# A decoder trunk's experts: copying the summed rows to the outputs before the last two blocks are added

## The reference, cut to what matters

```python
def moe(h, blk, w_router, router_bias, w_e_gate, w_e_up, w_e_down, w_s_gate, w_s_up, w_s_down):
    hf = h.reshape(B * S, D)
    eidx, gw = route(hf, w_router, router_bias)          # top 8 of 64 experts for each row
    routed = routed_experts(hf, eidx, gw, w_e_gate, w_e_up, w_e_down, blk)
    shared = swiglu(hf, w_s_gate, w_s_up, w_s_down)
    return (routed + shared).astype(h.dtype).reshape(B, S, D)

# routed_experts: pairs (row, expert) are sorted by expert and cut into blocks of one expert;
# a block's rows are gathered, go through its SwiGLU, are scaled by their weights and added:
    out = jnp.zeros((M + 1, D), ys.dtype).at[row_tok].add(ys * row_w[:, None])
```

## Time and profile before

| | |
|---|---|
| median of 3 runs | 2251.98 us (2250.02 to 2253.24) |
| span of the profiled execution | 2244.9 us |
| time around the span (median less span) | 7.1 us |
| busy: PE, DVE, ACT, POOL | 2097, 1345, 1050, 1023 us |
| experts' phase | from 1335.3 to 2244.9 us, 66 blocks |
| mean granted TensorE clock | 0.974 of full speed |

### The profile page before, as it was taken

One profiled execution on the slowest core, in us unless ns is written; L12 is line 12 of the kernel. 1 busy time (PEld: TensorE's weight loads), 2 busy tenths in 40 slices (PEclk: granted clock), 3 DMA queues, 4 the chain that ended last, 5 costly groups with the idle time before them and its releaser, 6 DMA issues. The chain is left out here.

```text
span 2244.9 us, 42905 instructions
## 1 busy us (share of the span) xinstructions
PE 2097.4 (93%) x15302; PEld 1583.8 (71%) x15302; DVE 1344.5 (60%) x2337; ACT 1050.3 (47%) x1584; POOL 1023.4 (46%) x850
## 2 busy tenths in 40 slices
PE   7998989979799989999898989999999999999994
PEld 6776767757444448888687647777777777777773
DVE  4478767675576662111357537777777777777772
ACT  6321213266566661111243216666666666666662
POOL 2111213252577741111015614567776676667662
PEclk9999999989899999999999999999999999999997
DMA  6577821064655556983342259999999999999996
GB/s 224 163 250 241 271 74 38 27 208 128 204 168 168 165 172 229 302 274 103 131 148 95 96 218 323 335 337 338 336 331 340 338 336 335 338 338 337 335 327 156
DMA packets 178690, 520.62 MB, mean 232 GB/s; under 512 B 22907, under 2 KB 77354, under 8 KB 152142
## 3 DMA queue, kind: packets, MB, share of 16 engines
q1 hardware_dynamic: 130070, 355.43, 45.2%
q0 software_dynamic: 37520, 97.81, 17.0%
q10 hardware_dynamic: 10992, 66.02, 8.7%
HBM read 442.31 MB, written 125.08 MB: 253 GB/s over the span
## 5 line engine op out<-in xcount | busy, mean ns | idle before, releaser
L2724 DVE TENSOR_TENSOR w_gu_lo<-turned,w_gu_hi 128x2048 fp32r<-128x2048 f32 x132 | 302.6, 2293 | 146.8 <-ACT w_gu_hi L2646 146.8
L2646 ACT ACTIVATE w_gu_hi<-turned 128x2048 fp32r<-128x2048 f32 x132 | 253.9, 1924 | 38.2 <-PEq L1926 38.2
L623 PE MATMUL pP<-wring,hT_hi 128*128 128x512 f32 (+1 forms) x576 | 225.9, 392 | 26.2 <-DVE wring L549 22.2
L625 PE MATMUL pP<-wring,hT_lo 128*128 128x512 f32 (+1 forms) x576 | 221.7, 385 | 0.0
L624 PE MATMUL pP<-wring,hT_hi 128*128 128x512 f32 (+1 forms) x576 | 221.4, 384 | 0.0
L2573 PE MATMUL pG_e<-w_gu_hi,xT_hi 128*128 128x512 f32 x528 | 214.7, 407 | 0.0
L2573 PE MATMUL pG_e<-w_gu_lo,xT_hi 128*128 128x512 f32 x528 | 209.0, 396 | 0.0
L2573 PE MATMUL pG_e<-w_gu_hi,xT_lo 128*128 128x512 f32 x528 | 208.6, 395 | 0.0
L2500 POOL DMA_INDIRECT x_scratch<-turned,target x66 | 106.8, 1619 | 205.9 <-ACT turned L2687 205.9
L389 POOL TENSOR_TENSOR wring<-turned,wring 128x512 fp32r<-128x512 f32 (+1 forms) x43 | 69.0, 1634 | 232.0 <-ACT wring L423 231.6
L2486 POOL DMA_INDIRECT turned<-h_scratch,index x64 | 159.0, 2484 | 20.0 <-issue 20.0
(11 more groups left out here) (335 smaller groups left out, 5030.3 us busy)
## 6 DMA issues: line engine op xcount, KB each, us to landing
turned<-in_w_e_up SPq DMA_DIRECT2D x65, 1024.0 KB, 11.2
turned<-in_w_e_down SPq DMA_DIRECT2D x65, 1024.0 KB, 6.8
turned<-in_cache_sb_kv SPq DMA_DIRECT2D x256, 256.0 KB, 3.1
turned<-in_w_e_gate SPq DMA_DIRECT2D x64, 1024.0 KB, 7.1
out<-in_cache_win_kv ACTq DMA_DIRECT2D x8, 4094.0 KB
turned<-in_w_in ACTq DMA_DIRECT2D x56, 256.0 KB, 7.0
turned<-in_w_in SPq DMA_DIRECT2D x16, 512.0 KB, 7.1
out<-in_cache_win_kv ACTq DMA_DIRECT2D x8, 1022.0 KB
```

The lines of the kernel that those rows point to most:

```text
L623: pe.matmul(pP[:m, i % 4, :w], hi, w_hi(u), start=(c == 0), stop=False)
L625: last = pe.matmul(pP[:m, i % 4, :w], lo, w_hi(u), start=False, stop=(c == KC - 1))
L2646: act.activation(ghi[:, r, k, :, :].rearrange("p c f -> p (c f)"), w[:, r, k, :], ACT.Copy).then_inc(ghi_ready, 1)
L2724: dve.tensor_tensor(glo[:, r, k, :, :].rearrange("p c f -> p (c f)"), w[:, r, k, :], ghi[:, r, k, :, :].rearrange("p c f -> p (c f)").bitc ...
```

## The change

The last two blocks (the last turn) are no longer added to x2 but to the outputs. SP waits only for `y_out` of the turns before (`last * 64`), and then issues all three copies of x2 to the outputs, both halves of the prompt among them; ACT issues none and waits for none.

POOL adds the last two blocks with a new `scatter_last`. The first of them waits for `copied` (48), the second for all of the first block's transfers. Each issues four indirect adding DMAs: rows and quarter rows to y_prompt, with bounds (an index from S on is skipped), and rows and quarter rows to y_sample, with indices that are smaller by S, where those of prompt rows have been pushed out of bounds by adding 65536. Padding slots are out of bounds in all four. The shifted indices are in a new SBUF tensor, `slot_decode`, which DVE computes at the end of `phase_out_route` with four instructions on 128 x 116 elements; POOL copies a block's pair of them to `target_decode` in a further small copy beside `aim`. The last block's results go to buffers of their own (`y_end`, `tail_end`, which are the row buffers of even blocks, free by then), so ACT's last put waits for no landing. A block of the last turn now adds 64 to `y_out`.

The diff, cut to its core:

```diff
@@ phase_out_route
+        beyond = sb("beyond", [P, 2, NBLK])
...
                     dve.tensor_tensor(x2[:m, t % 2, :], pY[:m, t % 2, :], x1_row(t), ALU.add).then_inc(x2_ready, 1)
+                for n, rows in enumerate((S, QT * S)):
+                    index = pT[:, n * P:n * P + NBLK]
+                    chain(dve.tensor_scalar(beyond[:, n, :], index, float(rows), float(FAR), ALU.is_lt, ALU.mult))
+                    chain(dve.scalar_tensor_tensor(slot_decode[:, :, n], index, -float(rows), beyond[:, n, :], ALU.add, ALU.add))
@@ phase_experts, SP
-                sp.wait_ge(y_out, last * (U * 32) + U * 32)
+                sp.wait_ge(y_out, last * (U * 32))
                 sp.dma_start(o[1][:, 0], sc["x2"][S:T, :]).then_inc(copied, 16)
-                sp.dma_start(half_rows(o[0][0], 0), half_rows(sc["x2"], 0)).then_inc(copied, 16)
+                for h in range(2):
+                    sp.dma_start(half_rows(o[0][0], h), half_rows(sc["x2"], h)).then_inc(copied, 16)
+                sp.wait_ge(y_out, last * (U * 32) + U * 64)
+                sp.nop(nofuse=True)
                 sp.wait_ge(copied, 48)
@@ POOL
+                def scatter_last(it, j):
+                    src, src_tail = (y, y_tail) if j == 0 else (y_end, tail_end)
+                    aim(it, j)
+                    pool.tensor_copy(target_decode[:, j, :], slot_decode[:, bass.ds(it * U + j, 1), :]).then_inc(decode_ready, 1)
+                    pool.wait_ge(target_ready, it * U + (j + 1))
+                    pool.wait_ge(decode_ready, j + 1)
+                    pool.wait_ge(y_copied, it * (2 * U) + 2 * (j + 1))
+                    if j == 0:
+                        pool.wait_ge(copied, 48)
+                    else:
+                        pool.wait_ge(y_out, it * (U * 32) + 64 * j)
+                    pool.nop(nofuse=True)
+                    for dst, at, rows_at, part in ((o[0][0], target, S, src), (out_quarters, target, QT * S, src_tail),
+                                                   (out_decode, target_decode, NS, src), (decode_quarters, target_decode, QT * NS, src_tail)):
+                        k = 1 if part is src_tail else 0
+                        pool.indirect_dma_start(dst, bass.IndirectOffsetOnAxis(ap=at[:, j, k:k + 1], axis=0), part, None,
+                                                bounds_check=rows_at - 1, oob_is_err=False, compute_op=ALU.add).then_inc(y_out, 16)
...
-                for n in range(LAG):
+                for n in range(1, LAG):
                     for j in range(U):
-                        aim(last - (LAG - 1 - n), j)
-                        scatter(last - (LAG - 1 - n), j)
-                pool.wait_ge(y_out, last * (U * 32) + U * 32)
+                        aim(last - n, j)
+                        scatter(last - n, j)
+                for j in range(U):
+                    scatter_last(last, j)
+                pool.wait_ge(y_out, last * (U * 32) + U * 64)
@@ ACT
+                def put_end(it):
+                    j = U - 1
+                    act.wait_ge(y_ready, it * U + (j + 1))
+                    act.wait_ge(target_ready, it * U + (j + 1))
+                    act.activation(y_end, pY[:, :], ACT.Copy, scale=scale[:, j % 2, 2:3]).then_inc(y_copied, 1)
+                    act.activation(tail_end, pQ[:, :QW], ACT.Copy, scale=scale[:, j % 2, 3:4]).then_inc(y_copied, 1)
...
-                put(last, U - 1)
-                act.wait_ge(y_out, last * (U * 32) + U * 32)
-                act.dma_start(half_rows(o[0][0], 1), half_rows(sc["x2"], 1)).then_inc(copied, 16)
-                act.wait_ge(copied, 48)
+                put_end(last)
```

More of the change, by code:

```diff
@@ L47 @@
 BIG = 1e30
+FAR = 1 << 16
 GATE_RING = 3
@@ L165, in build @@
             branches.close()
-            phase_out_route(nc, a, o, scratch, ident, turned, expert_row, slot_info)
-            phase_experts(nc, a, o, scratch, ident, turned, expert_row, slot_info)
+            slot_decode = attention.enter_context(nc.sbuf_tensor("slot_decode", [P, NBLK, 2], I32))
+            phase_out_route(nc, a, o, scratch, ident, turned, expert_row, slot_info, slot_decode)
+            phase_experts(nc, a, o, scratch, ident, turned, expert_row, slot_info, slot_decode)
 def phase_project(nc, a, o, sc, ident, turned):
@@ L1760, in expert_weights, with phase_out_route @@
     return a[name][0].rearrange("e (p c) f -> e p (c f)", p=P)[bass.ds(e, 1)].rearrange("e p n -> (e p) n")
-def phase_out_route(nc, a, o, sc, ident, turned, expert_row, slot_info):
+def phase_out_route(nc, a, o, sc, ident, turned, expert_row, slot_info, slot_decode):
     NC = T // 3
@@ L2343, in _, with phase_experts @@
                     dve.tensor_tensor(x2[:m, t % 2, :], pY[:m, t % 2, :], x1_row(t), ALU.add).then_inc(x2_ready, 1)
+                for n, rows in enumerate((S, QT * S)):
+                    index = pT[:, n * P:n * P + NBLK]
+                    chain(dve.tensor_scalar(beyond[:, n, :], index, float(rows), float(FAR), ALU.is_lt, ALU.mult))
+                    chain(dve.scalar_tensor_tensor(slot_decode[:, :, n], index, -float(rows), beyond[:, n, :], ALU.add, ALU.add))
                 dve.wait_ge(slots_ready, 4)
                 dve.wait_ge(row_ready, 2)
-def phase_experts(nc, a, o, sc, ident, turned, expert_row, slot_info):
+def phase_experts(nc, a, o, sc, ident, turned, expert_row, slot_info, slot_decode):
     U = TURN
@@ L2376, in phase_experts @@
         scale = target[:, :, :].bitcast(F32)
+        target_decode = sb("target_decode", [P, 2, 2], I32)
+        y_end, tail_end = rows[0], tail[0]
         xhi = sb("xT_hi", [P, 2, KC, P], F32R)
@@ L2420, in phase_experts @@
         copied = sem("c_copied")
+        decode_ready = sem("c_decode_ready")
+        out_quarters = o[0][0].rearrange("t (q n) -> (t q) n", q=QT)
+        out_decode = o[1].rearrange("t n d -> (t n) d")
+        decode_quarters = o[1].rearrange("t n (q d) -> (t n q) d", q=QT)
         def half_rows(ap, h):
```

## The result

| | before | after |
|---|---|---|
| median | 2253.3 us (20 runs) | 2259.15 us (20 runs) |
| ratio | | 1.0024, 95% interval 1.0018 to 1.0031 |
| span of the profiled execution | 2244.9 us | 2256.9 us |
| a block in the experts' loop | 13.247 us | 13.313 us |
| from block B's second scatter to the end | 41.1 us | 43.8 us |

The changed kernel is 5.4 us slower (0.0024 x 2253.3). The forecast was 2250.7 us, 1.3 us less than before. The profiled executions differ by 12.0 us: 5.2 of it is there already at the first block's gate (1349.8 us in before, 1354.9 us here), 4.1 comes in the loop over the blocks, 2.6 behind block B. The other two stay.

What follows compares the result with a forecast made beforehand. The end was taken as bound by the drain after PE's last matmul, 27.8 us of landings, POOL issues and copy. Drain sum 2242.8 plus 0.8 for bounds gave span 2243.6, plus 7.1 around it 2250.7 us; range 2246 to 2257.

Steps and rivals of the forecast that it cites:

- Step 1: In the final drain, SP issues the copy of x2 at 2208.7, 20.9 us earlier; it lands at 2223.8.
- Step 2: POOL waits for the copy's landing, so C, the second-to-last block, starts at 2224.6, 10.8 us later than before.
- 3, C's last transfer: On POOL, four transfers per block in place of two, spaced 1.88 us: 3.76 us more, for each last block.
- step 5: Pause from C's last start to D's (last block's) first: 3.69 us, POOL's aims just hidden, ACT's put off the path.
- 4, D landed: Each last block's final, nearly empty transfer lands 2.88 us after its start.
- Step 7: Check of bounds on POOL: 0.1 us more for each of eight transfers, 0.8 together, giving a span of 2243.6 us.
- Step 6: Sum of the drain: D's last transfer at 2239.6, landed 2242.5, end of span 2242.8 us.
- Step 8: Phase before the experts: DVE's four added instructions, some 1.6 us, are hidden under the last x2 row's store.
- rival of traffic: Skipped rows still cost DMA time as if moved, both last blocks DMA-bound: 4.1 us slower, 2256.1 us; chance 0.06.
- the faster: Rival: skipped rows are nearly free on POOL in the last blocks' transfers: span 2238.9, 2246.0 us; chance 0.15.
- slower rival: Bounded transfers take POOL 0.6 us longer each, eight on the path, with high landings: 2258.7 us; chance 0.17.
- the sign by which the prediction was to fail as a whole: POOL's cost per bounded transfer differs by more than 0.8 us from that of the unbounded one.

Runs made afterwards that it cites:

- e3: Kernel before with only the three new SBUF tensors allocated in their places, unused: 2255.76 us, ratio 1.0011, 13.313 us a block.
- e9: Changed kernel with slot_decode at the top of SBUF and target_decode behind all other tensors, so no tile moves: 2256.18 us, ratio 1.0005.
- e4: Changed kernel with POOL's aims of both last blocks ahead of the wait for the copy: 2258.65 us, ratio 1.0022 to the kernel before.
- e11: As e9, but without the four transfers to y_sample: 2252.25 us, ratio 0.9988 to the kernel before.
- e8: Changed kernel without POOL's own wait for the last landings: 2258.67 us, ratio 1.0020 to the kernel before.
- e10: As e9, with both aims early, no last wait on POOL, and D's first two transfers waiting only for C's first two: 2253.36 us, ratio 1.0000.

## Why the prediction was wrong

Against block B's second scatter (2203.81 in before, 2213.11 in after), the steps compare as follows.

| step | forecast | measured in after |
|---|---|---|
| 1, copy issued | 4.9 | 4.7 |
| 1, copy landed | 20.0 | 20.7 |
| 2, block C starts | 20.8 | 21.5 |
| 3, C's last transfer | 26.4 | 27.1 |
| 5, block D starts | 30.1 | 31.4 |
| 3, D's last transfer | 35.8 | 37.0 |
| 4, D landed | 38.6 | 39.7 |
| 7, check of bounds | 0.8 | 0 |
| 6, end of the span | 39.8 | 43.8 |

- Step 6 failed. "End of span" was put 0.37 us behind the last landing, because it is so in before. There, the last thing to land is a copy issued by SP and ACT, and POOL's drain of 3.49 us had ended 11 us before that. With POOL's own transfers last, the drain is exposed: 4.1 us from landing to end. This is 3.7 of the 4.0 us by which the end was missed. What step 5 names for the pause, "what is late next", no step names for the end of the kernel: the trace had the drain's length (L2430), and it was not read. It is a cover that was taken away unseen, while the copy it lay under was moved.
- The loop's 2.6 to 4.1 us were missed altogether. Step 8 is right about DVE: DVE's four instructions start at 1336.57 and the last ends at 1337.8, and ACT starts the experts 3.45 us behind the start of L2346, as 1331.88 and 1335.33 are apart in the earlier trace rows. But the prediction puts the two new tensors' place in SBUF at nothing, without a reason; its sign for step 8, that before 2200 no time should change, did fire. The allocation moved the tiles of the loop that PE bounds (e3, e9).
- Step 5 erred by 0.55 us. The sentence that ACT's put leaves the path was wrong: the put needs the second `aim` (it scales by its weights), and POOL got to that only behind C's transfers. Step 2 asked what is queued behind POOL's new wait, named the transfers, and forgot the aim and with it ACT. With the aim ahead, the pause is 3.52 us (e4), where 3.69 was forecast. The added small copy does not take as long again as the first, as step 5 has it: it starts 0.12 us behind it (2241.34 against 2241.22), which was not on the path.
- Step 1 was right in place and 0.8 us short in size: the copy took 15.97 us in place of 15.15, and 15.5 to 16.5 in the repeats, over the 16 us of its own sign in four of seven (0.7 are left behind block B, as it was issued 0.2 us sooner).
- Steps 2, 3 and 4 held: 0.84 us from the copy's landing to C (0.81 forecast), 1.86 us from transfer to transfer (1.88), 2.70 us from the last start to its landing (2.88).
- Step 7, the unknown on which the two main rivals rested, came out at nothing: 1.55 and 1.57 us for each of the eight, as without bounds, with nearly all rows skipped or nearly none. Nor is it so that a skipped row needs no descriptor, as far as packets tell: q0 has 576 packets more in the whole of after (38096 against 37520), which is 144 for each of the four transfers that are added; 408 to 451 of the 576 of one block are smaller than 512 B. They cost little time on the DMA engines: C's four transfers fill 33.9% of 10.4 us, 3.5 us, and D's 28.9% of 13 us, 3.8 us, where a pair of before fills 42.2% of 10 us, 4.2 us. So the rival of traffic, the faster and the slower rival are all out. That the slower rival's 2258.7 us lies near the 2259.15 measured is chance, and the sign by which the prediction was to fail as a whole, 0.8 us for a bounded transfer, did not come either.

The size of it all: 2.2 to 2.7 us from the end and 2.6 to 4.1 us from the loop make 4.8 to 6.8 us, where 5.4 were measured. The forecast's reason, that the 20.9 us by which the copy starts earlier are spent again by waiting and by eight transfers in a row, is borne out. Of the 4.0 us by which the end was missed, all but 0.3 are the drain; the copy's landing (0.7), the aim (0.6), the bounds (-0.8) and the rest (-0.2) nearly cancel, which is luck.

The Trainium skill (DMA: Bandwidth & Descriptors, Anatomy of one DMA — SWDGE (gpsimd) path) has a fixed cost of some 2 us for such a DMA. Here 2.70 us pass from the start of POOL's instruction to the landing of D's last, nearly empty transfer, 1.15 of them behind the instruction's end, so the forecast's 2.88 was nearer. What the section says on the small price of more descriptors these transfers do not test, as skipped rows had their packets too.

## What to carry to other kernels

When the last work of a kernel moves to another engine or queue, read what that engine does between its last transfer and the end, in the kernel before too, where it may lie under something. When a change allocates a tensor, even one that nothing in the hot loop uses, keep the loop's tiles where they were (put it last; a padding was not tried), and compare the loop's period before comparing anything else. And behind an engine's new wait list every instruction of that engine, the small copies that other engines wait for first of all.

## What the runs showed of the hardware

- Where a matmul's tiles lie in SBUF can cost PE time. A tensor of 16 bytes a partition in front of the rows' and hidden tiles made gate and up 5.705 us long in place of 5.688 and down 2.817 in place of 2.804, used or not, in six profiles of six. Together with 928 bytes in front of all tiles the block took 13.313 us in five profiles of five; with 16 alone 13.280, with 928 alone 13.260, with neither 13.247 or 13.271. The Trainium skill (SBUF — State Buffer, Operand start alignment) has the rule that an operand must start at a multiple of its element size, and says that this is about legality and not speed; the tiles moved by 16 bytes keep the rule, the outputs stay right, and the time changes.
- POOL's drain at the end of the experts takes 3.49 us where POOL has waited for the landing of two transfers a block (before, e11), 3.82 where it has waited for four (after), both counted from the landing, and 3.83 from the end of its last transfer's instruction where it does not wait (e8, e10). The other engines' drains at the same place took 1.3 us (DVE), 1.5 (ACT) and 0.007 (SP) in after.
- An indirect adding DMA with bounds occupies POOL for 1.55 to 1.57 us, as one without, also when nearly every row is skipped, and a skipped row still has its packet.
